# Other places for the lower weights and the inner activations' parts of feed-forwards 1 and 2

## The reference

```
def swiglu(x, w_gate, w_up, w_down):
    return (jax.nn.silu(x @ w_gate) * (x @ w_up)) @ w_down

f1 = swiglu(rms_norm(h, ffn1_pre_g[l]), ffn1_w_gate[l], ffn1_w_up[l], ffn1_w_down[l])
h = h + 0.5 * rms_norm(f1, ffn1_post_g[l])
mix = hybrid_mixer(...)                                # projections, two attentions, gates
h = h + rms_norm(mix, mix_post_g[l])
f2 = swiglu(rms_norm(h, ffn2_pre_g[l]), ffn2_w_gate[l], ffn2_w_up[l], ffn2_w_down[l])
h = h + 0.5 * rms_norm(f2, ffn2_post_g[l])
...                                                    # second block: three mixers
x = x + mod[5][:, None] * conv_ffn(h2, w_up[l], ffn_conv_w[l], w_down[l])   # feed-forward 3
```

## Time and profile before

| | |
|---|---|
| median of 3 runs | 1205.46 us (1203.77 to 1205.49) |
| span of the profiled execution | 1206.9 us |
| TensorE busy, weight loads busy | 98%, 92% |
| VectorE, ScalarE, GpSimd busy | 68%, 53%, 44% |
| mean granted TensorE clock | 0.987 |
| feed-forward 1, 2, 3 | about 10 to 190, 411 to 600, 1013 to 1203 us |

### The profile page before, as it was taken

How to read it: one execution, slowest core, us unless ns; L and a number is a source line. 1 busy time by engine, 2 the same in 40 slices (tenths; PEclk the granted TensorE clock), 3 DMA queues, 4 the chain that set the end, 5 groups by cost and what they waited for, 6 DMA issues and landing times.

```text
span 1206.9 us, 24404 instructions
## 1 busy us (share of the span) xinstructions
PE 1178.4 (98%) x9128; PEld 1111.1 (92%) x9128; DVE 816.0 (68%) x1121; ACT 637.3 (53%) x1018; POOL 527.1 (44%) x285
## 2 busy tenths in 40 slices
PE   6999999999999999999999999999999999999998
PEld 6999999987889899999999879987877999999998
DVE  7788875856865577777654852688836596655555
ACT  6444446525762555454546546468517635655553
POOL 0343436732465533343436645458530483232331
PEclk9999998999999999999989999999999999999999
DMA  6888884543334467878614333233323254666663
GB/s 221 277 278 294 283 280 130 190 140 123 105 108 137 157 210 259 292 274 292 188 52 158 123 99 129 88 106 105 105 70 106 88 175 140 208 185 188 188 189 121
DMA packets 58100, 207.10 MB, mean 172 GB/s; under 512 B 6576, under 2 KB 8240, under 8 KB 57776
## 3 DMA queue, kind: packets, MB, share of 16 engines
q1 hardware_dynamic: 49824, 177.23, 45.2%
q0 software_dynamic: 6912, 25.17, 5.7%
q10 hardware_dynamic: 1296, 3.74, 0.9%
HBM read 205.07 MB, written 1.05 MB: 171 GB/s over the span
## 4 chain that ended last, share of the span: by engine, by line
PE 82%; DVE 8%; issue 3%; ACT 3%; POOL 2%; DMA 1%; DVEq 0%; SPq 0%; POOLq 0%; ACTq 0%
PE psum L641 23%; PE psum L642 23%; PE psum L643 22%; POOL own_parts L2944 2%; PE psum L789 1%; PE psum L1017 1%; PE psum L942 1%; PE psum L652 1%; PE psum L654 1%; PE psum L653 1%; PE psum L666 1%; PE psum L1346 1%; POOL high L3039 1%; DVE u_parts L2882 1%; PE psum L700 1%
## 5 line engine op out<-in xcount | busy, mean ns | idle before, releaser
L641 PE MATMUL psum<-parts 128*128 128x256 f32 x1584 | 441.0, 278 | 14.0 <-DVE parts L2197 10.4
L642 PE MATMUL psum<-parts 128*128 128x256 f32 x1584 | 445.7, 281 | 0.0
L643 PE MATMUL psum<-parts 128*128 128x256 f32 x1584 | 441.6, 279 | 0.0
L641 PEld LDWEIGHTS psum<-parts 128*128 128x128 f32 x1584 | 299.5, 189 | 14.9 <-issue 11.0
L2952 POOL TENSOR_TENSOR parts<-low,parts 128x1024 fp32r<-128x1024 f32 x60 | 151.0, 2517 | 367.4 <-ACT parts L1520 367.4
L643 PEld LDWEIGHTS psum<-parts 128*128 128x128 f32 x1584 | 299.7, 189 | 0.0
L642 PEld LDWEIGHTS psum<-parts 128*128 128x128 f32 x1584 | 299.7, 189 | 0.0
L1520 ACT ACTIVATE parts<-low 128x1024 fp32r<-128x1024 f32 x198 | 207.4, 1056 | 163.1 <-DMA low<-stream 162.4
L2944 POOL TENSOR_TENSOR own_parts<-low,parts 128x1024 fp32r<-128x1024 f32 x75 | 184.9, 2479 | 151.5 <-ACT parts L1598 147.4
L2197 DVE TENSOR_TENSOR parts<-low,parts 128x1024 fp32r<-128x1024 f32 x138 | 163.6, 1219 | 23.6 <-ACT parts L1520 22.9
L642 PE MATMUL psum<-u_parts,parts 128*128 128x256 f32 (+1 forms) x560 | 164.7, 294 | 0.0
(11 more groups left out here) (384 smaller groups left out, 2091.1 us busy)
## 6 DMA issues: line engine op xcount, KB each, us to landing
low<-stream SPq DMA_DIRECT2D x334, 512.0 KB, 3.6
high<-conditioning POOLq DMA_DIRECT2D x48, 512.0 KB, 5.0
high<-wuq ACTq DMA_DIRECT2D x1, 1152.0 KB, 5.1
low<-x SPq DMA_DIRECT2D x4, 256.0 KB, 6.3
high<-ctx ACTq DMA_DIRECT2D x1, 1024.0 KB, 6.4
out<-low SPq DMA_DIRECT2D x8, 128.0 KB, 1.8
low<-cst ACTq DMA_DIRECT2D x1, 850.5 KB, 4.8
low<-vec ACTq DMA_DIRECT2D x1, 157.5 KB, 6.3
```

The lines of the kernel that those rows point to most:

```text
L641: pe.matmul(out, w_hi[:, cols_], x_hi, start=start, stop=False, **kw)
L642: pe.matmul(out, w_hi[:, cols_], x_lo, start=False, stop=False, **kw)
L643: return pe.matmul(out, w_lo[:, cols_], x_hi, start=False, stop=stop, **kw)
```

## The change

Five numbers of the table of starts change. No instruction is added, removed or put in another order on any engine; only addresses change, in feed-forwards 1 and 2. The lower weights begin half a line off instead of on a line; in feed-forward 1 both parts of `hidden` then begin at 0 modulo 256; in feed-forward 2 they change places, 128 for the upper and 0 for the lower part.

```diff
-PART_STARTS = ({"ring_lo": 16, "u_hi": 112, "u_lo": 16, "hidden_hi": 112, "hidden_lo": 144},
-               {"ring_lo": 16, "u_hi": 112, "u_lo": 80, "hidden_hi": 112, "hidden_lo": 144},
+PART_STARTS = ({"ring_lo": 0, "u_hi": 112, "u_lo": 16, "hidden_hi": 112, "hidden_lo": 176},
+               {"ring_lo": 32, "u_hi": 112, "u_lo": 80, "hidden_hi": 144, "hidden_lo": 176},
                {"ring_lo": 16, "u_hi": 112, "u_lo": 80, "hidden_hi": 112, "hidden_lo": 208})
```

## The result

The changed kernel's median is 1215.73 us (11 runs, 1214.31 to 1217.4), that of the kernel before 1207.08 us (11 runs beside them, 1203.77 to 1217.05). The ratio is 1.0062, with a 95% interval of 1.0043 to 1.0081 (the medians alone would give 1.0072). The forecast was 1202.0 us and its range ended at 1207.5: wrong in sign, and out of the range. The time came out on the side of the rival that I called the slow pace.

A forecast was written before the change was run, and what follows sets the result against it. TensorE's pace per triple was taken to bound the kernel. Lower weights off the line were to save 3.5 us, with hidden parts, writers, transfers and clock at nothing: 1205.5 - 3.5 = 1202.0 us, range 1198.0 to 1207.5.

The forecast's parts named there:

- the slow pace: Rival: triples in feed-forwards 1 and 2 settle at 353.3 ns, 7.0 us more, 1212.5 us; chance 0.15, in all or part.
- What bounds the kernel: Whole kernel: TensorE, busy 98% of the span; a feed-forward costs its number of triples times the 346.7 ns pace.
- Writers: VectorE, GpSimd and ScalarE writing lower weights and hidden parts to other places: costed at nothing.
- the time between 1 and 2: Sign between feed-forwards 1 and 2: a change of more than a microsecond would prove the forecast wrong.
- the first term: Lower weights, feed-forwards 1 and 2: step 642 to 643 falls from 118.3 to 115 ns, 3.5 us less over 1056 triples.
- Hidden parts: Activations streamed in down, feed-forwards 1 and 2: no price in 1, no change taken in 2.
- The bounds: Limits of the lower-weights term: 340 to 353.3 ns a triple, from 7.0 us less to 7.0 us more.
- Quick pace: Rival: all steps in feed-forwards 1 and 2 fall to 113 ns, 7.0 us less, 1198.4 us; chance 0.15.
- Distance: Rival: only weights 64 bytes behind the streamed operand's place are quick; net gain 0.3 us, 1205.2 us; chance 0.13.
- Places indifferent: Rival: places don't matter, the 118.3 ns step comes from matmul order; triple stays 346.7 ns, 1205.5 us; chance 0.12.

The follow-up runs named there:

- e1: Against the kernel before, only the lower weights moved: to 64 in feed-forward 1, 192 in 2, modulo 256 bytes; 1216.74 us, ratio 1.0066.
- e8: The changed kernel with 128 instead of 256 columns streamed in all gate, up and down blocks but the first of each sum; 1416.53 us.
- e3: Against the kernel before, all three feed-forwards with both activation parts at 0 and all weights at 64; 1210.87 us, ratio 1.0014.
- e2: Against the kernel before, only the hidden parts moved: both at 0 in feed-forward 1, upper 128 and lower 0 in 2; 1207.76 us, ratio 0.9983.
- e4: Against the kernel before, all weights at 64 and both activation parts together at 64, 128, 192 in feed-forwards 1, 2, 3; 1221.04 us, ratio 1.0101.
- e7: One more execution of the e3 kernel, with nothing changed; 1205.25 us.
- e9: Against the kernel before, gate and up have activations at 0 and weights at 64, while down keeps the old places; 1203.65 us, ratio 0.9971.
- e10: Mirror of e9: down has activations at 0 and weights at 64, gate and up keep the kernel before's places; 1209.39 us, ratio 1.0008.
- e12: Against the kernel before, activations at 0 and weights at 64 almost everywhere; only down of every second chunk keeps the old places; 1204.89 us, ratio 0.9962.
- e5: The e3 kernel with the lower hidden part of every second chunk at 128 instead of 0; 1211.04 us, ratio 1.0042 against the kernel before.
- e6: The kernel before run and profiled once more, with nothing changed; 1206.94 us.

## Why the prediction was wrong

**What bounds the kernel** was right: the change moved the time by TensorE's pace and by nothing else of size. Writers cost next to nothing (the two waits in feed-forward 2), and feed-forward 3 kept its pace. That the time between 1 and 2 would stay within a microsecond was narrowly missed (+1.4).

**The step that failed** is the first term, "two loads on a line cost 3.3 ns each, so 118.3 becomes 115". It took the output projection's difference of 6.6 ns for the price of a load by its own address, and carried it to another load. What the runs showed instead: with the lower weights off the line the step from 642 to 643 went from 118.3 to 117.9 ns in feed-forward 1, which is 0.4 of the 3.3 ns; the two steps that I held untouched rose, 641 to 642 from 113.4 to 118.0, and 643 to 641 from 115.0 to 117.1. In feed-forward 2 all three rose, to 119.2, 122.8 and 120.3. e1 has that loss with the weights alone, and e8 shows that a load's address has no price without a long stream beside it. The two rows compared in the forecast differed in one address, but also in which pair of load and stream met, and I read only the first. The term of -3.5 us came out as +7.8 us, all of it gate and up, since the two `down` cancel; its mechanism was wrong, not only its size.

**Hidden parts: "the price is none."** In feed-forward 1 the argument, streams from 0 beside weights at 64, led to the quick cell, and `down` came at 340.6 ns, 2.8 ns below the forecast's 343.4. It also came out so only because that cell was in its quick state: e3 shows 353.4 for it. In feed-forward 2, where I took no change, `down` cost 6.3 ns more: each step is within my bounds of 113.3 to 118.3, but all three are near the upper one (117.5, 117.9, 117.6). With the old weights the same hidden parts made `down` slower, not equal (e2).

**The bounds were too narrow.** I bounded the triple by 340 and 353.3 ns, the quickest and slowest rows of the trace. Two thirds of feed-forward 2 came at 362.3, outside both. The nearest rows bound a cost only if they vary the thing that is changed; none had weights at 192.

**The rivals.** Quick pace: right for `down` of feed-forward 1, wrong elsewhere. Distance: it foresaw that feed-forward 1's `down` is quick and feed-forward 2's is slow, and its 340 ns cell is real, but gate and up of 2 should have gained and lost most. Places indifferent: refuted by 340 to 363 ns, and with it what I drew from the Trainium skill ("SBUF — State Buffer", "Who interferes with whom"), that with two independent read ports and no waiting for anyone the pace would not depend on places. e8's loads alone do fit it, the full streams don't; whether it is the ports that load and stream share isn't shown. Slow pace: the right sign and nearly the size, 7.0 us forecast and 7.1 us between the profiles, but the size was luck: it had 353.3 ns in all of both feed-forwards, and of the four kinds of triple only two came near that, one was at 340.6 and one at 362.3. I priced it by the right warning, "one placement shows two paces, and a placement that the trace lacks can fall on either", and then gave it 0.15, since in the trace the slow pace appeared only where all weights lie on a line. That evidence was three placements out of many, and should have weighed less.

**What is shown and what is open.** Shown: the pace belongs to the whole cell of places (e1, e2, e4); one cell, (0, 0 | 64, 64), has two states that last through continuous work and, as long as that cell alone runs, change only at an interruption (e3, e7); a tile with the kernel before's places leads into the quick state and one with (0, 0 | 64, 128) into the slow one (e9, e10, e12), one with (0, 128 | 64, 64) leaves it as it is (e5); the effect is an overlap of load and long stream (e8 with e1). Open: the rule that gives the pace from the four places, how the state is chosen behind an interruption, and which resource the load and the stream share. The wide spread of runs (1203.77 to 1217.05 for the kernel before itself) is open too. Its two profiles, before and e6, have the same paces and differ in waits for `hidden_lo` and in slow stretches of the clock; what these do in the other runs wasn't measured.

## What to carry to other kernels

Where TensorE loads weights and streams for about as long, the places of both operands modulo 256 bytes can be worth some per cent of its pace (340 to 363 ns a triple here), and they must be measured as a combination: one address can't be priced from a row in which the other operand lay elsewhere. A placement that shows two paces in one trace is a warning that its gain may not hold, so look at a second execution and at what follows each interruption, and each stretch with other places, before counting on it. When the bounding engine is made quicker, look for who must now keep up, here a subtraction on VectorE that waits behind GpSimd's.

## What the runs showed of the hardware that I had not expected

- One placement runs at 340.0 or at 353.3 ns a triple, for a hundred microseconds on end, with instructions and addresses the same (e3, e7).
- Between the placements tried here the triple ranges from 340.0 to 362.7 ns; with streams of 128 columns the cells of e8 all take about 335 ns.
- Which pace such a placement has can be set by the tile before it: 128 of 128 tiles behind before's places were quick, nine of nine behind (0, 0 | 64, 128) slow (e9, e10, e12).
- With these shorter streams the granted clock stood at 0.50 for all of 100 us, though TensorE counts as busy for 100 of them, 470 matmuls about 213 ns apart (e8's window row); yet in e8's feed-forward 3 it stood at 1.00 for 160 us. With 256 columns the low level came for some 3 to 10 us at a time, the start of feed-forward 2 included (granted clock 0.56 from 419 to 426 us in the kernel before).
- A 128x256 subtraction on VectorE, 425 ns alone, takes up to 1.55 us beside GpSimd's subtraction of 2.4 us.
